# A conditioned hybrid encoder layer on one core: the first bias addition of the next neighbourhood head between the last two dot products, and the first turned low part ahead of a weight piece's low part, on VectorE

## The reference, cut to what matters

```python
mod = silu(c) @ w_ada + b_ada                      # 6 x 2048 numbers: shifts, scales, gates
h = rms_norm(x, g1) * (1 + sc1) + sh1              # 512 tokens x 2048
proj = h @ w_in                                    # q, k, v of 8 neighbourhood and 8 differential heads
na_o = rms_norm(neighbourhood_attention(q, k, v, rpb))   # softmax(q k^T * s + bias, -inf outside a window) v
da_o = rms_norm(differential_attention(q, k, v, t5, lam))
x = x + g1 * (concat(na_o, da_o) @ w_out)
x = x + g2 * ((silu(h2 @ w_gate) * (h2 @ w_up)) @ w_down)
return rms_norm(x, final_g)
```

## Time and profile before

| | |
|---|---|
| median of three runs | 2240.65 us (2238.47 to 2241.41) |
| profiled execution: time, and span of its trace | 2239.34 us, 2237.8 us |
| busy: TensorE, VectorE, ScalarE, GpSimd | 2178.6, 1735.0, 882.6, 257.0 us |
| the eight neighbourhood steps, from the first block of scores of step 1 to the first of step 9 | 202.98 to 417.02 us |
| granted clock of TensorE, mean over the span | 0.991 |

### The profile page before, as it was taken

How to read it: one execution, slowest core, us unless ns; L and a number is a source line. 1 busy time by engine, 2 the same in 40 slices (tenths; PEclk the granted TensorE clock), 3 DMA queues, 4 the chain that set the end, 5 groups by cost and what they waited for, 6 DMA issues and landing times. The chain is left out here.

```text
span 2237.8 us, 32734 instructions
## 1 busy us (share of the span) xinstructions
PE 2178.6 (97%) x10966; PEld 1822.7 (81%) x10966; DVE 1735.0 (78%) x2438; ACT 882.6 (39%) x1235; POOL 257.0 (11%) x311
## 2 busy tenths in 40 slices
PE   7999999999999999999999999999999999999996
PEld 4878888777777887888888888888888787888885
DVE  6976677777876989789888888898888654999333
ACT  4224333455444214444444444444444432444221
POOL 4012222100004331000000000000000100000221
PEclk9999999999999999999999999999999999999998
DMA  9895666533525983333333333333333643435332
GB/s 334 295 357 167 210 207 211 185 129 131 184 97 190 344 284 118 107 114 117 127 126 117 115 125 117 117 126 127 117 118 118 236 150 114 131 108 173 94 98 100
DMA packets 136136, 360.15 MB, mean 161 GB/s; under 512 B 21945, under 2 KB 50761, under 8 KB 135569
## 3 DMA queue, kind: packets, MB, share of 16 engines
q1 hardware_dynamic: 124498, 319.08, 42.1%
q0 software_dynamic: 10576, 40.18, 5.0%
q10 hardware_dynamic: 1008, 0.21, 0.0%
HBM read 340.23 MB, written 19.18 MB: 161 GB/s over the span
## 5 line engine op out<-in xcount | busy, mean ns | idle before, releaser
L1594 DVE TENSOR_TENSOR W_lo<-raw,W_hi 128x1024 fp32r<-128x1024 f32 (+1 forms) x192 | 234.7, 1223 | 176.3 <-ACT W_hi L1104 176.1
L1104 ACT ACTIVATE W_hi<-raw 128x1024 fp32r<-128x1024 f32 (+1 forms) x192 | 196.3, 1023 | 433.1 <-PE T L690 111.8
L2110 DVE TENSOR_TENSOR W_lo<-raw,W_hi 128x1024 fp32r<-128x1024 f32 x192 | 234.7, 1222 | 56.3 <-ACT W_hi L1419 52.3
L1419 ACT ACTIVATE W_hi<-raw 128x1024 fp32r<-128x1024 f32 x192 | 203.1, 1060 | 172.6 <-PE P L996 93.6
L2113 DVE TENSOR_TENSOR raw<-raw 128x1024 f32<-128x1024 f32 x192 | 233.9, 1219 | 0.0
L1419 ACT ACTIVATE H<-raw 128x1024 fp32r<-128x1024 f32 x144 | 152.1, 1056 | 171.1 <-DVE raw L2113 98.3
L996 PE MATMUL P<-H,W_hi 128*128 128x512 f32 x768 | 192.4, 392 | 1.7 <-issue 1.7
L688 PE MATMUL PS<-H,W_hi 128*128 128x512 f32 x416 | 169.1, 406 | 17.9 <-POOL ident L2485 10.8
L688 PE MATMUL P<-H,W_hi 128*128 128x512 f32 x432 | 176.9, 409 | 1.9 <-DVE H L2066 1.2
L2110 DVE TENSOR_TENSOR H<-raw,H 128x1024 fp32r<-128x1024 f32 x144 | 175.5, 1219 | 0.0
L690 PE MATMUL P<-H,W_lo 128*128 128x512 f32 x432 | 169.2, 392 | 0.0
(11 more groups left out here) (318 smaller groups left out, 4409.3 us busy)
## 6 DMA issues: line engine op xcount, KB each, us to landing
raw<-in_w_gu SPq DMA_DIRECT2D x176, 512.0 KB, 3.2
raw<-in_w_in SPq DMA_DIRECT2D x72, 512.0 KB, 3.4
adar<-in_w_ada SPq DMA_DIRECT2D x72, 512.0 KB, 4.4
att<-in_w_ada SPq DMA_DIRECT2D x32, 1024.0 KB, 10.6
att<-in_w_ada SPq DMA_DIRECT2D x56, 512.0 KB, 4.8
raw<-in_w_out SPq DMA_DIRECT2D x32, 512.0 KB, 4.8
raw<-in_w_down SPq DMA_DIRECT2D x32, 512.0 KB, 3.4
raw<-in_w_down SPq DMA_DIRECT2D x32, 448.0 KB, 3.3
```

The costliest lines, as they stand in the source:

```text
L1104: act.activation(w_parts(slot)[0][:, 0:cols], raw[:, raw_slot * PW:raw_slot * PW + cols], ACT.Copy).then_inc(hi_done, 1)
L1419: act.activation(form_parts(FORM_SLOT[a])[0], raw_form(FORM_RAW[a]), ACT.Copy).then_inc(hi_done, 1)
L1594: dve.tensor_tensor(lo[:, 0:cols], raw[:, raw_slot * PW:raw_slot * PW + cols], hi[:, 0:cols].bitcast(F32), ALU.subtract).then_inc(lo_done, 1)
L2110: dve.tensor_tensor(lo, raw_form(FORM_RAW[a]), hi.bitcast(F32), ALU.subtract).then_inc(lo_done, 1)
```

## The change

Two operations of VectorE's `na_step4` stand elsewhere; nothing is added or removed. The bias of block 0 of the next neighbourhood head was the first operation of a step, behind the dot products and `keep` of the step before; it now stands in the step before, between its fifth dot product (number 4) and its sixth (number 5). Step 1 keeps its own at the start, and step 8 has no neighbourhood head behind it, so seven of the eight (heads 1 to 7) move. And `turned_low_na(a, 0)`, the low part of the first half of the turned probabilities, now stands ahead of the low part of weight piece 3, in all eight steps.

```diff
--- before.py
+++ after.py
@@ -1714,8 +1714,9 @@
                 dve.wait_ge(ada_dot, u + each)
                 dve.tensor_copy(modp[:, bass.ds(u + 64, each)], st[:, 0:each]).then_inc(kept, 1)
 
-            def na_step4(p, a, pkind):
-                bias_scores(a, "na", 0)
+            def na_step4(p, a, pkind, begin=False):
+                if begin:
+                    bias_scores(a, "na", 0)
                 split_head(p, 1, 4)
                 bias_scores(a, "na", 1)
                 ada(p, "na4", 0)
@@ -1728,14 +1729,16 @@
                 ada(p, "na4", 1)
                 q_low(p, Pb[0], pkind)
                 k_low(p, key_land)
+                turned_low_na(a, 0)
                 split_head(p, 3, 4)
-                turned_low_na(a, 0)
                 ada(p, "na4", 2)
                 turned_low_na(a, 1)
                 ada(p, "na4", 3)
                 split_head(p + 1, 0, 4)
                 take_o(a, "na")
                 ada(p, "na4", 4)
+                if pkind == "na":
+                    bias_scores(p, "na", 0)
                 ada(p, "na4", 5)
                 keep(p, "na4")
 
@@ -1941,7 +1944,7 @@
             q_low(0, Pb[0], "na")
             k_low(0, key_land)
             split_head(1, 0, 4)
-            na_step4(1, 0, "na")
+            na_step4(1, 0, "na", True)
             with dve.Fori(2, NAH) as p:
                 na_step4(p, p - 1, "na")
             na_step4(NAH, NAH - 1, "da")
```

## The result

The changed kernel takes **2246.36 us** (median of 9 runs, 2244.45 to 2253.91) where the kernel before takes 2241.09 (9 runs, 2237.93 to 2244.93): **1.0024 times**, 95% interval 1.0015 to 1.0032. So the change costs 5.3, 3.4 and 2.9 us, about 3.9 in the mean. The forecast was +1.5 (2242.0) and a range up to 2245.2: the sign and the places were right, the size was too small, and the first measurement fell outside the range. The two repeats, 2243.92 and 2243.85, lie inside it.

A forecast was written before the change was run, and what follows sets the result against it. Two equally long loops bound it: TensorE's 26.13 us and VectorE, SyncE's queue and transfers, 26.10. The earlier bias gives -3.8, the turned low part takes 5.3: 1.5 us later, 2242.0 us; own range 2239.7 to 2244.6, wider range 2237.3 to 2245.2.

The forecast's parts named there:

- What bounds the kernel: Attention part: TensorE's loop without waits, 26.13 us a step, and a VectorE, SyncE-queue and transfer loop, 26.10, are equally long.
- The earlier bias: Bias between fifth and sixth dot products: TensorE's block 2 waits vanish; this edit alone gives -3.8 us.
- Rival 2: VectorE's moved bias waits for GpSimd's square: seven times 0.46 = +3.2 us, 2245.3; chance 0.10.
- The turned low part: Ahead of piece 3's low part on VectorE: delays it 1.08 us, or 0.60 where k's low part is late.
- rival 1: Fourth dot product's landing doesn't move, so the turned low part costs nothing: -3.8, 2236.9 us; chance 0.12.
- rival 3: Piece 3's low part to next piece 0's gives back half its delay; edits cancel within 1.5 us: 2239.5; chance 0.10.
- the second loop: VectorE, SyncE's queue and transfers: 26.10 us a step becomes 26.70 with the turned low part, passing TensorE's 26.13.
- The first mark: Low part of weight piece 0 ending step 1, where TensorE is ahead: 1.08 us later.
- last seven legs: Stretches from piece 3's low part to the next low part of piece 0, over seven steps: 64.44 us together, unchanged.
- the delay stays to the end: Behind step 9 TensorE waits for little until the next stage, so the 1.5 us delay remains in the total.
- TensorE's piece 0: TensorE waits for piece 0's low part until 1.4 us after that starts: 0.5 to 2 us in steps 2, 3, 7, 8.
- Block 3's wait: TensorE's block 3 of the scores waits for block 1's bias: 0.14 us, swallowed by the loop's slack.

The follow-up runs named there:

- Experiment 2: Only the earlier bias, the turned low part back behind piece 3's low part, against the changed kernel: 2236.66 us, 0.9985 of the kernel before.
- experiment 4: Changed kernel (both edits) with the fourth dot product's load issued ahead of the reload of slot 3 and the key: 2236.86 us, 0.9984 of the kernel before.
- experiment 6: Kernel before, neither edit, with the fourth dot product's load issued ahead of the reload of slot 3 and the key: 2236.39 us, 0.9978 of before.
- experiment 7: Only the earlier bias, plus the fourth dot product's load ahead of reload and key: 2235.30 us, 0.9975 of the kernel before.
- experiment 3: Only the turned low part ahead of piece 3's low part, the bias left in place, against the kernel before: 2250.71 us, 1.0049 times.

## Why the prediction was wrong in size, point by point

**What bounds the kernel: right.** Two loops of equal length. Experiment 2 takes the waits of one away and falls on the other (26.29 a step); experiments 4, 6 and 7 shorten the other and fall on TensorE's 26.13.

**The earlier bias, -3.8 us: right,** -3.9 measured alone (1.1 to 5.4 by the interval), seven steps 184.0 for 183.6. That the sizes agree to 0.1 is luck: in its one trace the mark of step 9 is only 2.7 ahead of the mean of before (411.53 against 414.27). It takes the place foreseen, mark + 2.9, and is 0.35 long beside GpSimd's square. Rival 2, that it waits for GpSimd, is refuted: `keep` and the low part behind it stay at mark + 6.03. By the section of the Trainium skill that the prediction weighed (SBUF — State Buffer, "Who interferes with whom") it should pass, since the scores come from PSUM; the traces agree, 0.35 with GpSimd busy and 0.35 or 0.36 without (0.36 in experiment 7).

**The turned low part: its price in place was right,** 0.61 where the second loop sets the pace. The leg starts later and gives nothing back, so rivals 1 and 3 (the landing doesn't move, or by half) fall: legs 9.45, 9.20 and 9.40 with both edits, 9.17 with this one alone, against 9.22, 9.35 and 8.98. Half elastic, this one alone would have had legs of 8.6 (9.18 less half of 1.08). The prediction didn't have the third loop of experiment 3, since there the early bias opens it; it decides nothing in the changed kernel.

**The step that failed is the sum "So the second loop is 26.10 + 0.60 = 26.70 ... Seven steps: 7 x 17.48 + 64.44 + 0.97 = 187.8, against 187.35: +0.4", with "The first mark ... +1.08".** The mechanism was right; each term was sized from one execution, and the sum came out at 1.5 us where the marks show 3.55. Over three executions each:

| term | forecast | measured, means of three |
|---|---|---|
| first mark, later by | 1.08 | 228.75 - 227.32 = 1.43 |
| mark to piece 3's low part, seven steps | 123.3 | 123.70, 123.70, 124.69: 124.0 |
| last seven legs | 64.4 | 66.12, 64.10, 64.91: 65.0 |
| seven steps of before | 187.35 | 187.35, 188.06, 185.45: 186.95 |
| mark of step 9, later by | 1.5 | 417.82 - 414.27 = 3.55 |

0.35 + 0.7 + 0.6 + 0.4 is the 2.05 that was missing.

The second term is the landing of the second dot product. I had let it be late once, as in step 2 of before; in the first execution of after it is late by 1.25 in step 5, in the second by 0.9 in step 3, in the third by about 0.9 in steps 3 and 7. What I overlooked is what a late landing costs. The kernel before, in step 4 of its third execution, and the changed kernel, in step 3 of its second (second dot product, k's low part, what follows it):

```profile
295.63 1.23 DVE L1603 CUSTOM_DVE_ANT_0 adar<-adar,csb 128x1024 f32<-128x1024 f32 x1 [0.93 <-DMA adar<-in_w_ada]
...
297.38 0.68 DVE L1686 TENSOR_TENSOR k_lo<-raw,split_att 128x512 fp32r<-128x512 f32 x1
298.13 1.23 DVE L1594 TENSOR_TENSOR W_lo<-raw,W_hi 128x1024 fp32r<-128x1024 f32 x1
```

```profile
270.60 1.23 DVE L1603 CUSTOM_DVE_ANT_0 adar<-adar,csb 128x1024 f32<-128x1024 f32 x1 [1.19 <-DMA adar<-in_w_ada]
...
272.95 0.68 DVE L1674 TENSOR_TENSOR split_att<-T,split_att 128x512 fp32r<-128x512 f32 x1
273.55 1.21 DVE L1594 TENSOR_TENSOR W_lo<-raw,W_hi 128x1024 fp32r<-128x1024 f32 x1
```

Before, the dot product starts at mark + 15.02, 0.56 late, and piece 3's low part at mark + 17.52. There it stands in 19 of 21 steps before (17.49 to 17.55), and in step 3 it was released by ScalarE's high part (272.49), so the first 0.6 of a delay costs nothing. After, the turned low part has taken up that slack: the dot product at mark + 15.33 gives the low part at mark + 18.28, the delay goes to the next mark in full, and from there into TensorE's wait (1.69 in step 6). Over seven steps the low part is late by 0.3, 0.1 and 0.4 us in all before (against 17.51 a step), by 1.3, 1.3 and 2.3 after (against 17.48).

The first, third and fourth terms are scatter of executions, which I had taken at 1.2 us for the legs and given, as the forecast's tail, only 0.05 of the chances to a time above 2245.1. No run shows a cause for them. How much of the 3.55 is the kernel and how much the draw stays open: executions of one kernel differ by 2.5 and 3.0 us at that mark, though the two sets don't touch (412.8 to 415.3, 416.2 to 419.2). The six traced executions lie 5.8 us apart in the mean (2239.4 and 2245.2), more than the 3.9 of the medians, so the traces rather overstate the loss.

**From the mark to the end: "the delay stays to the end", right.** The next mark, of step 10, is later by 3.5 as well (441.42, 441.96, 439.42 before; 444.75, 442.84, 445.83 after), and so is the end of the last head's wait, some 250 us on. In the times it is 3.9 over the three comparisons. The first comparison's 5.3 is the highest of them.

**The other signs.** TensorE's piece 0 at mark + 1.27 (forecast 1.4), "0.5 to 2 us in steps 2, 3, 7 and 8" against 0.17 to 0.44 in six and 1.69 and 1.07 in two, steps 6 and 9: right in kind, wrong in place. Block 3's wait is only in the weight loads, 2.0 us in 7, 0.3 each.

The DMA page of the Trainium skill (DMA: Bandwidth & Descriptors, "Measured") gave an estimate of 3.8 us for the 1.31 MB; the changed kernel's trace has 6.69 from the reload to the dot product in step 3. The measurement decides: no part of the leg came back.

## What to carry to other kernels

When two loops over different engines are equally long, an edit that shortens one is worth only what the other allows, and one that lengthens either costs in full; work out every cycle through the schedule, with and without each edit, since one edit can open a loop that another closes (here, in the stretch up to piece 3's low part, -3.8 and +7.8 us alone and +1.2 together). Look at what is queued ahead of the load that the loop waits for before reordering the compute around it: moving that one load ahead of a reload and a key that nobody was waiting for gave 0.2% and left both edits worth nothing that could be measured. Where a step waits on transfer landings, size it from several executions, let the chances carry their scatter, and look for what slack took up a late landing before: an edit that uses up the slack makes every late landing count.

## What the runs showed of the hardware that was not expected

- After a wait of 3.1 us of TensorE at the last head's mixing the granted clock in 690 to 700 us is 0.83, 0.83, 0.83, 0.85 and 0.66 in five executions of the two kernels, and the mixing takes 8.0 us, or 8.6 with 0.66, instead of 6.5; after a wait of 1.52, in the sixth, it is 1.00. That sixth had its lower clock 20 us earlier, behind a wait of 2.21 us that ended at 676.26; the same wait, 2.19 to 2.21 us, left the clock at 1.00 in the other five. What decides that isn't shown.
- A copy of six columns on VectorE lasts 0.17 us, or 1.03 until GpSimd's operation ends, six times as long.
- In step 3 a 512 KB load behind a 512 KB reload and a 256 KB key is there 6.69 us after the reload's issue, and behind the reload alone 5.12; the legs that hold these loads differ by 1.4 in the mean of eight steps.
